# Stick-breaking mixers: keys and the second half of the queries computed with the weight blocks stationary

## The reference

```python
def stick_breaking_mixer(xn, w_qkv, w_o):
    b, s, _ = xn.shape
    qkv = (xn @ w_qkv).reshape(b, s, 3, SB_HEADS, SB_HEAD_DIM)
    q, k, v = [qkv[:, :, i].transpose(0, 2, 1, 3).astype(jnp.float32) for i in range(3)]
    ...
        z = jnp.einsum('bhqd,bhkd->bhqk', qb, k) * scale
        mask = key_pos[None, :] < q_pos[:, None]
        log_beta = jax.nn.log_sigmoid(z)
        log_1m_beta = jnp.where(mask, jax.nn.log_sigmoid(-z), 0.0)
        suffix = lax.cumsum(log_1m_beta, axis=3, reverse=True) - log_1m_beta
        weights = jnp.where(mask, jnp.exp(log_beta + suffix), 0.0)
        return jnp.einsum('bhqk,bhkd->bhqd', weights, v)
```

## Time and profile before

| what | value |
|---|---|
| time, median of 3 runs | 1723.64 us (1723.12 to 1724.19) |
| the profiled execution | 1722.8 us, of it the span 1721.0 us |
| PE, DVE, ACT, POOL busy | 1713.3, 1217.4, 1045.3, 167.1 us |
| stick-breaking stage of layer 0 | about 560 to 665 us of the span |
| that of layer 3 | about 1419 to 1524 us |

### The profile page before, as it was taken

How to read it: one execution, slowest core, us unless ns; L and a number is a source line. 1 busy time by engine, 2 the same in 40 slices (tenths; PEclk the granted TensorE clock), 3 DMA queues, 4 the chain that set the end, 5 groups by cost and what they waited for, 6 DMA issues and landing times. The chain is left out here.

```text
span 1721.0 us, 22917 instructions
## 1 busy us (share of the span) xinstructions
PE 1713.3 (100%) x8786; PEld 1431.1 (83%) x8786; DVE 1217.4 (71%) x1680; ACT 1045.3 (61%) x1623; POOL 167.1 (10%) x137
## 2 busy tenths in 40 slices
PE   9999999999999999999999999999999999999998
PEld 8888887788888878888888888888888888788887
DVE  7867667667777778766667766588776666786664
ACT  7665667757565766654565744477665446665542
POOL 0000011200000010211000210002021100102110
PEclk9999999999999999999999999999999999999999
DMA  9555453255555533555544555453455554336552
GB/s 366 202 196 185 174 204 141 86 190 220 185 186 186 190 124 122 210 193 196 189 187 165 217 187 186 166 208 147 159 208 196 187 181 183 133 112 222 187 192 72
DMA packets 45997, 311.62 MB, mean 181 GB/s; under 512 B 5472, under 2 KB 5856, under 8 KB 9664
## 3 DMA queue, kind: packets, MB, share of 16 engines
q1 hardware_dynamic: 45328, 309.00, 49.2%
q0 software_dynamic: 272, 1.05, 0.2%
q10 hardware_dynamic: 288, 0.11, 0.0%
HBM read 309.09 MB, written 1.05 MB: 180 GB/s over the span
## 5 line engine op out<-in xcount | busy, mean ns | idle before, releaser
L1397 DVE SCALAR_TENSOR_TENSOR wlo<-raw,first,whi 128x512 fp32r<-128x512 f32 x704 | 505.7, 777 | 108.5 <-ACT whi L746 108.0
L746 ACT ACTIVATE whi<-raw,first 128x512 fp32r<-128x512 f32 x704 | 452.8, 713 | 85.0 <-PE ps L2304 72.0
L2403 PE MATMUL ps<-xs,whi 128*128 128x512 f32 x1344 | 423.2, 396 | 0.0
L2302 PE MATMUL ps<-whi,xs 128*128 128x512 f32 (+1 forms) x896 | 358.6, 400 | 0.4 <-DVE wlo L1397 0.4
L2304 PE MATMUL ps<-whi,xs 128*128 128x512 f32 (+1 forms) x896 | 348.6, 389 | 0.0
L2303 PE MATMUL ps<-wlo,xs 128*128 128x512 f32 (+1 forms) x896 | 347.8, 388 | 0.0
L2406 PEld LDWEIGHTS ps<-xs,wlo 128*128 128x128 f32 x1344 | 252.4, 188 | 59.3
L2302 PE MATMUL ps<-whi,hhi 128*128 128x512 f32 x720 | 281.3, 391 | 0.0
L2303 PE MATMUL ps<-wlo,hhi 128*128 128x512 f32 x720 | 280.4, 389 | 0.0
L2304 PE MATMUL ps<-whi,hlo 128*128 128x512 f32 x720 | 280.2, 389 | 0.0
L1394 DVE TENSOR_TENSOR wlo<-raw,whi 128x2048 fp32r<-128x2048 f32 x110 | 250.8, 2305 | 26.9 <-ACT whi L737 26.9
(11 more groups left out here) (251 smaller groups left out, 1355.0 us busy)
## 6 DMA issues: line engine op xcount, KB each, us to landing
raw<-in_w_parts SPq DMA_DIRECT2D x283, 1024.0 KB, 4.8
gain<-in_gains SPq DMA_DIRECT2D x10, 512.0 KB, 6.4
raw<-in_w_parts SPq DMA_DIRECT2D x5, 512.0 KB, 8.5
x<-in_x SPq DMA_DIRECT2D x2, 512.0 KB, 10.5
arena<-in_bias_line POOLq DMA_DIRECT2D x1, 1024.0 KB, 13.1
out<-x SPq DMA_DIRECT2D x4, 256.0 KB, 2.0
proj<-in_x_turned SPq DMA_DIRECT2D x2, 256.0 KB, 4.0
raw<-in_w_parts SPq DMA_DIRECT2D x2, 256.0 KB, 4.0
```

The lines of the kernel that those rows point to most:

```text
L746: nc.scalar.activation(whi[n % HIS][:, cols], raw[n % LOS][:, cols], ACT.Copy, scale=gcol[:, COLUMNS[n] + kk:COLUMNS[n] + kk + 1]).then_in ...
L1397: nc.vector.scalar_tensor_tensor(out=lo[:, cols], in0=whole[:, cols], scalar=gcol[:, COLUMNS[n] + kk:COLUMNS[n] + kk + 1], in1=hi[:, cols] ...
L2302: nc.tensor.matmul(out_ap, a_hi, wh, start=first, stop=False)
L2403: nc.tensor.matmul(ps[:, 4 + m, :], whi[n % HIS][:, kk * BANK + m * P:kk * BANK + (m + 1) * P], xs[:, k, :, :].rearrange("p h n -> p (h n) ...
```

## The change

Jobs 2, 3 and 4 (k first half, q second half, k second half) of the two stick-breaking projections become weight-stationary (`turned_job`): per part and per pair of 128-column blocks (u = 0 into banks 4, 5; u = 1 into banks 0, 1), eight k in two halves. Their results already have the head dimension on partitions, so `sb_turn` and `sb_copy` remain for b = 0, 1 alone. Instead ACT copies the lower half of the banks (`sb_lower`), DVE adds the upper (`sb_sum`) and POOL multiplies by the row of scales (`scaled`). A job's second use of a pair of banks waits for that pair's `sb_sum`. The orders of ACT, DVE and POOL are rewritten around it.

```diff
# PE
+                def turned_job(j):
+                    for jj, n in enumerate(parts_of(j)):
+                        for u in range(2):
+                            if jj == 0 and j > 2:
+                                pe.wait_ge(tile_summed, 6 * s["n_sb"] + 2 * (j - 3) + u + 1)
+                            elif jj == 0 and u == 0:
+                                pe.wait_ge(lin_evac, base + 1)
+                            for kk in range(PANELS):
+                                k = PANELS * jj + kk
+                                between(mix, j, jj, PANELS * u + kk)
+                                if u == 0:
+                                    weights(n, kk)
+                                for m in range(2):
+                                    at = kk * BANK + (2 * u + m) * P
+                                    nc.tensor.matmul(ps[:, (4, 0)[u] + m, :], whi[n % HIS][:, at:at + P],
+                                                     xs[:, k, :, :].rearrange("p h n -> p (h n)"), start=(k == 0), stop=False)
+                                for m in range(2):
+                                    at = kk * BANK + (2 * u + m) * P
+                                    ins = nc.tensor.matmul(ps[:, (4, 0)[u] + m, 0:SEQ], wlo[n % LOS][:, at:at + P],
+                                                           xhi[:, k, :], start=False, stop=(k == KT - 1))
...
+                    rows_of_scales(s)
+                    for j in (2, 3, 4):
+                        turned_job(j)
...
+                        if s["woven_kind"] == "mix_sb":
+                            pe.wait_ge(tile_summed, 6 * s["n_sb"] + 5)
...
# sb_between
-                if at == (2, 1, 5):
+                if at == (2, 0, 6):
                     sb_turn(s, 0)
                     sb_turn(s, 1)
-                elif at == (3, 0, 2):
-                    sb_turn(s, 2)
...
-                    sb_turn(s, 3)
-                    sb_turn(s, 4)
...
-                    sb_turn(s, 5)
...
-                    sb_turn(s, 6)
...
-                    sb_turn(s, 7)
...
# ACT
+            def sb_lower(s, b):
+                act.wait_ge(job_done, s["n_job"] - 12 + nth_job(b // 2 + 1, b % 2))
+                nc.scalar.activation(tile_rows(b), split_banks(b, 1), ACT.Copy).then_inc(lower_ready, 1)
...
+                nc.scalar.activation(ROW, ps[:, 3, 0:SEQ], ACT.Copy)
+                nc.scalar.activation(ROW_Q, ps[:, 3, 0:SEQ], ACT.Copy, scale=0.125).then_inc(row_ready, 1)
+                hi_to(part0 + 8, 2)
+                sb_copy(s, 0)
                 hi_to(part0 + 9)
-                evac(2, 0)
+                sb_lower(s, 2)
                 hi_to(part0 + 10)
...
+                sb_lower(s, 3)
+                hi_to(part0 + 11, 2)
+                sb_lower(s, 4)
                 hi_to(part0 + 12)
...
+                sb_lower(s, 5)
                 sb_exp(s, 0)
                 sb_log(s, 0)
-                evac(4, 0)
-                hi_to(part0 + 14)
+                hi_to(part0 + 13)
+                sb_lower(s, 6)
                 sb_exp(s, 1)
                 sb_log(s, 1)
-                evac(4, 1)
+                sb_lower(s, 7)
                 sb_exp(s, 2)
                 sb_log(s, 2)
                 hi_to(part0 + 15)
-                sb_copy(s, 6)
                 sb_weights(s, 0)
# DVE
+            def sb_sum(s, b):
+                dve.wait_ge(lower_ready, 6 * s["n_sb"] + b - 1)
+                nc.vector.tensor_tensor(tile_rows(b), split_banks(b, 0), tile_rows(b), ALU.add).then_inc(tile_summed, 1)
...
+                lo_to(part0 + 8, 2)
+                sb_copy(s, 1)
+                lo_to(part0 + 9)
+                sb_sum(s, 2)
                 lo_to(part0 + 10)
+                sb_sum(s, 3)
+                lo_to(part0 + 11, 2)
                 sb_masked(s, 0)
                 sb_negated(s, 0)
+                sb_sum(s, 4)
+                lo_to(part0 + 12)
+                sb_sum(s, 5)
                 lo_to(part0 + 13)
+                sb_softplus(s, 0)
                 sb_masked(s, 1)
                 sb_negated(s, 1)
+                sb_sum(s, 6)
+                sb_low(s, 0)
+                sb_masked(s, 2)
+                sb_negated(s, 2)
+                sb_sum(s, 7)
+                sb_softplus(s, 1)
             def mix_sb(s, part0):
                 sb_masked(s, 3)
                 sb_low(s, 1)
+                lo_to(part0 + 2)
+                sb_softplus(s, 2)
                 sb_arg(s, 0)
-                sb_softplus(s, 2)
+                sb_low(s, 2)
                 sb_arg(s, 1)
-                sb_low(s, 2)
-                sb_copy(s, 5)
...
# POOL
+                def scaled(b):
+                    pool.wait_ge(tile_summed, 6 * s["n_sb"] + b - 1)
+                    row = ROW_Q if b in (4, 5) else ROW
+                    nc.gpsimd.tensor_tensor(tile_rows(b), tile_rows(b), row.unsqueeze(1).to_broadcast([P, 2, SEQ]), ALU.mult
+                                            ).then_inc(tile_scaled, 1)
...
+                for b in range(2, 6):
+                    scaled(b)
+                rounded(0)
+                scaled(6)
+                rounded(1)
+                scaled(7)
+                for p in range(2, 8):
+                    rounded(p)
```

More of the change, by code:

```diff
@@ L92, in stage_list @@
                           "ht", "gw", "rows", "sb", "qk", "qka", "qkd", "rms", "var", "br")}
-    for s in st:
+    for s, following in zip(st, st[1:] + [None]):
         s.update({"n_" + k: v for k, v in run.items()})
@@ L126, in stage_list @@
         if kind == "lin":
-            run["lin"] += 2 * s["doubles"]
+            run["lin"] += 3 if following["kind"] == "mix_sb" else 2 * s["doubles"]
+            run["rows"] += following["kind"] == "mix_sb"
             run["job"] += 4 * s["doubles"]
@@ L435, in build @@
         row_ready = sem("row_ready")
+        lower_ready = sem("lower_ready")
+        tile_summed = sem("tile_summed")
+        tile_scaled = sem("tile_scaled")
         tcopy_ready = sem("tcopy_ready")
@@ L555, in turned_tiles, with split_banks, tile_rows @@
             return arena[:, first:first + 512]
+        def split_banks(b, lower):
+            first = 4 if b % 2 == 0 else 0
+            return ps[:, first:first + 2, SEQ * lower:SEQ * (lower + 1)]
+        def tile_rows(b):
+            return turned_tiles(b).rearrange("p (m n) -> p m n", m=2)
         def swish_half(t, half):
@@ L1135, in sb_copy @@
                 act.wait_ge(qk_tr, s["n_qk"] + b + 1)
-                nc.scalar.activation(turned_tiles(b), ps[:, b % 2, :], ACT.Copy, scale=0.125 if b % 4 < 2 else 1.0
+                nc.scalar.activation(turned_tiles(b), ps[:, 2 + b, :], ACT.Copy, scale=0.125 if b % 4 < 2 else 1.0
                                      ).then_inc(qk_act, 1)
@@ L2240, in mix_sb, with rounded @@
                 p0 = 8 * s["n_sb"]
-                for p in range(8):
+                pool.wait_ge(row_ready, s["n_rows"])
+                def scaled(b):
[3 more added lines that the diff above has]
+                                            ).then_inc(tile_scaled, 1)
+                def rounded(p):
                     pool.wait_ge(n_ready, p0 + p + 1)
@@ L2372, in first_jobs, with rows_of_scales @@
                 counted_job(1, bank_of(1, 1), parts_of(1))
+            def rows_of_scales(s):
+                pe.wait_ge(norm_ready, s["norms"])
+                for t in range(NT):
+                    ins = nc.tensor.transpose(ps[:, 3, t * P:(t + 1) * P],
+                                              stat[:, RS, ROW_NORM + t:ROW_NORM + t + 1].to_broadcast([P, P]), ident)
+                ins.then_inc(row_ps, 1)
             def ffn(s, gated):
@@ L2380, in ffn @@
                 kind_turned = s["kind"] in TURNED_KINDS
[L2382 to L2388, removed]
                 def up_turned(i, j, u):
@@ L2518, in parts_of @@
                     return [part0 + 2 * j, part0 + 2 * j + 1]
-                first_jobs(s, lin_bank, parts_of)
-                for j in range(2, jobs):
+                def turned_job(j):
[18 more added lines that the diff above has]
+                                                           xhi[:, k, :], start=False, stop=(k == KT - 1))
+                            if jj == 1:
+                                ins.then_inc(job_done, 1)
+                            elif u == 1:
+                                ins.then_inc(w_used, 1)
+                first_jobs(s, lin_bank, parts_of)
+                if s["woven_kind"] == "mix_sb":
+                    rows_of_scales(s)
+                    for j in (2, 3, 4):
+                        turned_job(j)
+                for j in range(5 if s["woven_kind"] == "mix_sb" else 2, jobs):
                     for t in range(NT):
-                        if tight and j > 2:
+                        if s["woven_kind"] == "mix_sb":
+                            pe.wait_ge(tile_summed, 6 * s["n_sb"] + 5)
+                        elif tight and j > 2:
```

55 lines of the change are left out of this document (16 added, 39 removed).

## The result

The kernel after takes 1728.88 us (median; 1726.16 to 1733.74 over 12 runs), the kernel before, on the same chip, 1723.61 us (1722.48 to 1724.47, 12 runs): a ratio of 1.003, interval 1.0021 to 1.0039. It is 5.3 us slower, where 1.6 us were forecast (1725.2 us), and 0.9 us above the upper end of the 80% range (1728.0 us). The spread of the kernel after is 7.6 us where the kernel before has 2.0, and that is the first thing to explain.

A forecast was written before the change was run, and what follows sets the result against it. PE alone was taken to bound the kernel. Per stage, -1.64 of PE work, +0.25 at addition 3 and +2.18 at the seam gave +0.79, for two +1.6, so 1725.2 us; 80% range 1720.3 to 1728.0.

The forecast's parts named there:

- What bounds the kernel: Both stick-breaking stages: PE alone sets the end; less PE work shortens it one for one, waits cost their full length.
- addition 3: DVE's sum that PE needs for job 3's second pass; ends at 597.20, making PE wait about 0.25 us a stage.
- PE's own work: Per stage: transposes removed -2.68, weight-stationary form +0.82, transposes of the scales +0.22, together -1.64 us.
- third rival: The weight-stationary form costs less or more than in an MLP: 1723.6 us at nothing, 1726.8 at double; chance 0.05.
- second collision: Another POOL row product beside DVE's work ahead of a bank hand-over, 1.05 us of further PE wait.
- second rival: Banks handed over late at job 3's second pass; one more collision per stage adds 2.1 us, 1727.3 us; chance 0.17.
- The seam: PE's suffix sum of pair 1 waits for DVE's argument 0, ending at 629.22: a wait of 2.18 us a stage.
- two bounds: PE's wait before suffix sum 1: 1.45 us from ACT's high half of p13, 2.18 with POOL's row product, which was taken.
- lower bound: PE's wait before suffix sum 1 set by ACT's late high half of p13, without POOL's product: 1.45 us.
- first rival: Both waits vanish if DVE reaches p13's low half earlier, only PE's work counts: -3.3 us, 1720.4 us; chance 0.18.
- closing sum: Both stages: +0.79 us each, +1.6 together; profiled execution 1724.4, plus 0.84 to the median, gives 1725.2 us.

The follow-up runs named there:

- 8: Kernel after with panel p13 split a job earlier on ACT and DVE, otherwise the order of 7: 1721.18 us, ratio 0.9989 to the kernel before.
- 3: Kernel after with the low half of panel p13 moved on DVE from ahead of softplus 2 to behind negation 3: 1722.55 us, ratio 0.9996.
- 7: Kernel after with argument 0 right behind pair 1's low half, p13's low half as in 3, addition 3 ahead of p9's last panel: 1722.31 us, ratio 0.9993.
- 6: Kernel after with POOL's row product 7 moved behind the high half of pair 2: 1724.79 us, ratio 1.0007.
- 9: Kernel of 8 with 96 satisfied semaphore waits more on PE in the MLPs of the first and second layer: 1720.18 us, ratio 0.9982.
- 5: Kernel before with 48 satisfied semaphore waits more on PE in the first layer's MLP, nothing else: 1724.44 us, ratio 1.0007.
- 2: Kernel after, unchanged, run and profiled once more: 1728.98 us, ratio 1.0032 to the kernel before.
- 4: Kernel before with only the low half of panel p13 moved on DVE to just ahead of argument 0, making PE wait: 1728.8 us, ratio 1.0035.

## Why the prediction was wrong

**What bounds the kernel: right.** PE alone sets the end, and each wait in its order is paid in full, and somewhat over: a comparison of 8 with after, start by start, has the wait at addition 3 at 0.41 us, since the matmul behind it comes 0.10 later as well.

**PE's own work: right.** -1.64 us a stage were forecast, -1.63 and -1.67 measured where next to nothing waits (8), -1.64 in 3 and -1.83 in 7 with their waits taken off, so it holds to 0.2 us. So the third rival, another price of the form, is out.

**Addition 3: right.** DVE's walk gave its end 597.20; the profiled start lies 0.94 later, so 598.14, and it ended at 598.15. The wait was 0.31 instead of 0.25. No second collision came; the second rival is out.

**The seam: right in each member, 0.23 short.** Argument 0 should have ended at 629.22 + 0.94 = 630.16 and ended at 630.27. The hand-over to PE, which I had put at 0.03, takes 0.14 here (630.27 to 630.41; 627.28 to 627.42 in 3), though only 0.05 at addition 3 (598.15 to 598.20). That was to be read from before: argument 0 ended at 627.81 and the sum started at 627.97, and I called those 0.16 us slack where nearly all of it was the hand-over. The argument itself came 0.11 later than walked; that makes the 0.23. The two bounds are shown by 6: POOL's product costs 0.80, and without it the wait is 1.60, against the lower bound of 1.45.

**The first rival** (both waits vanish) did not happen in the change, but 8 is that rival made: both halves of p13 earlier, -3.3 us over the stages as worked out. Its time of 1720.4 was met only when the third layer was put right too, 1720.18 in 9.

**The step that failed is the closing sum**: "Per stage -1.64 + 0.25 + 2.18 = +0.79, for two +1.6 us. The profiled execution ... becomes 1724.4; it lay 0.84 under the median of the runs, which becomes 1725.2." It takes the rest of the kernel to stay as it was, and the median to lie as far above a profile as before, so it puts two terms at nothing without a reason: what the change does outside the two stages, and what a wait of PE does to TensorE's clock. Neither is nothing. To the 1725.2 come:
- 0.5 us from the stages' sizes (2.04 instead of 1.58), about half of it the hand-over.
- 1.0 us in the third layer (+1.00 in the profile; +1.15 in 5, with none of the change). A code packet falls into a burst of loads. That the position of the code decides is shown by 5, which brings the delay in with nothing of the change, and by 9, which takes it out with all of the change there.
- the lower clock. A stretch costs 1.55 us in 2 and 1.57 in 4. The median run of the kernel after is at 0.998 or 0.997, one or two stretches slower than its best runs, so an estimated 1.6 to 3.1 us; what the sum leaves is 1728.9 - 1725.2 - 0.5 - 1.0 = 2.2. That the wait brings it is shown by 4 (the wait without the change: all 5 runs at 0.998 or 0.997) and by 3, 6, 7, 8 and 9 (the change with that wait shortened or gone: 54 of 55 runs at 0.999 or more, where the kernel after has 12 of 18 below). The exception is the run of 3 at 1725.09.

The forecast gave 0.71 to a time within 0.2% of before and 0.18 to a slower one, and it came out 0.3% slower. The sizes and the third layer alone would have left it within (1726.7 us, 3.1 above before); it was the clock that took it out.

I had taken the wait of PE at its length. In this kernel, where TensorE otherwise never rests, two waits of 2.4 us cost 2 x 2.4 and on the median some 2 us more: as an estimate the wait's true price is about 1.4 of its length, and 4 agrees (5.6 us for 4.1 us of wait). By the Trainium skill (TensorE: Matmul & The Clock Gate, Part 1) idleness brings the array's clock to half rate; the rows of 2 and 4 agree, 0.50 behind the wait and 1.00 ahead of it, though the section speaks of longer idleness than the 2.06 and 2.41 us here, and there the measurement decides.

**What stays open.** What decides whether a given wait brings the lower clock: the waits of 2.41 us did so in one stage of four profiled ones, those of 2.06 in one of two, those of 1.60 in neither of two and, by spread and clock, in none of 11 runs. These are the cases seen, no law. Two of the 69 runs of the kernel before beside the experiments were at 0.998 too, with 1725.92 and 1726.92 us, and so was one of the 10 of 5 (1726.84 us); with the run of 3 that makes four. So the lower clock can come without such a wait, but seldom. Nor was it seen how the run of 1733.74 us at 0.994 came about. And how one packet of 16 KB makes a load of 1 MB late (7.6 to 8.1 us from issue to landing instead of 6.4 to 6.6) was not seen, only that it does when it starts 15 us after the mark, among the loads, and not at 3 us, ahead of them. By the view of queue 8 (0.3% of 16 engines' time over 19.5 us) the packet itself takes about 0.9 us, which is near the delay; whether that is the reason no run shows.

## What to carry to other kernels

On an engine that never rests, a wait of some 2 us that is put in can cost more than its length (here about 1.4 of it), so price it once with and once without the fall of the clock, and read the end of such a change from the spread and the granted clock of the runs before its median. Walk the other engines instruction by instruction, as that gave the times at the seam and at addition 3 to about 0.1 us here, take the hand-over between two engines from a row in which one waits for the other, and ask of a large instruction on the way (2.29 us here) not where it is hidden in the old order but where the new order has that much room. And compare the stages that the change does not touch: if a load comes later there, look for code packets in its burst before you look for a cause in the change.

## What was not expected of the hardware

- 48 instructions that do nothing, added to PE's stream in the first layer, made the third layer 1.15 us longer (97.16 to 98.31 us); 96 others took 1.7 us out of it (98.61 to 96.92).
- After a wait of 2.06 or 2.41 us TensorE ran 3.4 us at a granted clock of 0.50 in two of six profiled cases, starting 1.6 and 1.7 us after it had begun to work again, at a cost of 1.55 and 1.57 us.
- The start of the kernel, up to the first mark, takes 186.7 to 188.3 us by chance, whatever the kernel, and is no part of a change.
